# A turned tile read back from ScalarE's queue instead of SyncE's, with two other moves, in a two-layer decoder trunk

## What is computed

```
for l in range(2):
    x = LN1(alpha*x + 0.5*swiglu(x, ffn1_w_gate[l], ffn1_w_up[l], ffn1_w_down[l]))
    x = LN2(alpha*x + hybrid_mixer(x, w_in[l], ...))
    x = LN3(alpha*x + 0.5*swiglu(x, ffn2_w_gate[l], ffn2_w_up[l], ffn2_w_down[l]))

swiglu(x, g, u, d) = (silu(x @ g) * (x @ u)) @ d
```

## Time and profile before

| what | value |
|---|---|
| median of 3 runs | 1085.61 us (1084.34 to 1086.91) |
| profiled execution, its own time | 1085.02 us |
| its span | 1083.2 us |
| PE busy | 1074.1 us (99%) |
| VectorE busy | 772.2 us (71%) |
| ScalarE busy | 579.4 us (53%) |
| mean granted clock of TensorE | 0.998 |

### The profile page before, as it was taken

The page is one execution under the profiler, slowest core; times in us unless marked ns, Lnnn a source line. Parts: engine busy times, 40 slices in busy tenths (PEclk is TensorE's granted clock), DMA queues, the critical chain, the costliest instruction groups (busy, mean ns, idle before and its releaser), DMA issues.

```text
span 1083.2 us, 14466 instructions
## 1 busy us (share of the span) xinstructions
PE 1074.1 (99%) x5293; PEld 888.2 (82%) x5293; DVE 772.2 (71%) x773; ACT 579.4 (53%) x641; POOL 134.4 (12%) x137
## 2 busy tenths in 40 slices
PE   9999999999999999999999999999999999999997
PEld 6888888898888788888888888888988888888886
DVE  5747557799979775555679575677999787755566
ACT  5646654768555544444457555547774546444441
POOL 1397000000000000000006970000000000000000
PEclk9999999999999999999999999999999999999999
DMA  8767778355566477767737777785455674777771
GB/s 284 246 207 250 263 246 235 111 180 173 172 186 203 156 263 233 233 221 259 255 120 246 240 237 233 247 203 165 147 165 157 194 269 134 235 240 234 234 244 39
DMA packets 192371, 226.38 MB, mean 209 GB/s; under 512 B 31541, under 2 KB 157129, under 8 KB 192329
## 3 DMA queue, kind: packets, MB, share of 16 engines
q1 hardware_dynamic: 192328, 225.83, 65.5%
HBM read 214.26 MB, written 11.53 MB: 208 GB/s over the span
## 4 chain that ended last, share of the span: by engine, by line
PE 97%; DMA 1%; DVE 1%; ACT 0%; SPq 0%; issue 0%; DVEq 0%; ACTq 0%
PE ps L589 25%; PE ps L566 19%; PE ps L568 18%; PE ps L567 18%; PE ps L549 2%; PE ps L990 1%; PE ps L992 1%; PE ps L991 1%; PE ps L537 1%; PE ps L538 1%; PE ps L539 1%; PE ps L551 1%; PE ps L604 1%; PE ps L920 1%; PE ps L697 0%; PE ps L696 0%
## 5 line engine op out<-in xcount | busy, mean ns | idle before, releaser
L1471 DVE TENSOR_TENSOR w_lo<-raw,w_hi 128x2048 fp32r<-128x2048 f32 x172 | 399.8, 2328 | 167.7 <-ACT w_hi L1074 167.0
L1074 ACT CAST w_hi<-raw 128x2048 fp32r<-128x2048 f32 x172 | 328.2, 1911 | 170.4 <-PE ps L589 81.0
L566 PE MATMUL ps<-w_hi,xT 128*128 128x512 f32 x848 | 331.8, 391 | 0.3 <-DVE w_lo L1483 0.2
L567 PE MATMUL ps<-w_lo,xT 128*128 128x512 f32 x848 | 330.1, 389 | 0.0
L568 PE MATMUL ps<-w_hi,xT 128*128 128x512 f32 x848 | 330.1, 389 | 0.0
L566 PEld LDWEIGHTS ps<-w_hi,xT 128*128 128x128 f32 x848 | 159.2, 188 | 35.9 <-issue 2.5
L568 PEld LDWEIGHTS ps<-w_hi,xT 128*128 128x128 f32 x848 | 159.2, 188 | 33.5
L567 PEld LDWEIGHTS ps<-w_lo,xT 128*128 128x128 f32 x848 | 159.2, 188 | 32.6
L589 PE MATMUL ps<-w_hi,rows_hi 128*128 128x512 f32 x396 | 126.7, 393 | 0.3 <-DVE rows_lo L1520 0.2
L589 PE MATMUL ps<-w_hi,rows_lo 128*128 128x512 f32 x396 | 125.4, 390 | 0.0
L589 PE MATMUL ps<-w_lo,rows_hi 128*128 128x512 f32 x396 | 125.4, 389 | 0.0
(11 more groups left out here) (251 smaller groups left out, 1209.0 us busy)
## 6 DMA issues: line engine op xcount, KB each, us to landing
raw<-in_ffn_w_down SPq DMA_DIRECT2D x44, 1024.0 KB, 6.3
raw<-in_ffn_w_gate SPq DMA_DIRECT2D x86, 512.0 KB, 4.0
raw<-in_ffn_w_up SPq DMA_DIRECT2D x86, 512.0 KB, 5.2
raw<-in_w_in SPq DMA_DIRECT2D x30, 1024.0 KB, 5.1
hid_dram<-qT SPq DMA_DIRECT2D x160, 64.0 KB, 2.4
qT<-hid_dram SPq DMA_DIRECT2D x40, 256.0 KB, 2.6
raw<-in_w_out SPq DMA_DIRECT2D x8, 1024.0 KB, 4.8
raw<-in_w_in SPq DMA_DIRECT2D x8, 512.0 KB, 4.8
```

Source lines behind the costliest of these rows:

```text
L566: mm(o, xT[:, c, 0, tok], h, start=c == UPPER_FIRST[0], stop=False, skip_group_check=True)
L567: mm(o, xT[:, c, 0, tok], w, start=False, stop=False, skip_group_check=True)
L1074: nc.scalar.copy(w_hi[s][:, :], raw[s][:, :]).then_inc(hi_made.sem, 1)
L1471: tt(w_lo[s][:, :], raw[s][:, :], f32(w_hi[s][:, :]), ALU.subtract).then_inc(lo_made.sem, 1)
```

## The change

Three things are changed. (1) The read-back of the turned values is issued by ScalarE instead of SyncE. ScalarE waits for the four block writes and issues the DMA at the start of each step, ahead of the down chunk's cast; SyncE goes on from the block writes to the next load. (2) The loads of the norm's scale and shift move from behind the last loop of SyncE to between steps 7 and 8. (3) In the last step of an FFN the silu of the first token tile moves ahead of the cast of the next part's first chunk (`split_first`), where something follows.

```diff
                     sp.dma_start(hid_dram.rearrange("g i a r -> a i g r")[a],
                                  hid_blocks[32 * a:32 * a + 32, :].rearrange("i (g r) -> i g r", g=4)
                                  ).then_inc(blocks_out.sem, 16)
-                sp.wait_ge(blocks_out.sem, blocks_out.at(l, n))
-                sp.dma_start(hid_turned, hid_dram.rearrange("g i a r -> (g i) (a r)")).then_inc(h_turned.sem, 16)
...
                 after_steps()
-                with sp.Fori(5, STEPS) as i:
+                with sp.Fori(5, 8) as i:
                     step(i)
-                before_last()
+                norm_vectors()
+                with sp.Fori(8, STEPS) as i:
+                    step(i)
                 load(l, k0 + FFN_CHUNKS - 1, rows(w_down, l, DFF - 256))
                 turn_hidden(l, (f + 1) * (STEPS - 1))
...
+            def read_back(l, n):
+
+                sc_.wait_ge(blocks_out.sem, blocks_out.at(l, n))
+                nc.scalar.dma_start(hid_turned, hid_dram.rearrange("g i a r -> (g i) (a r)")).then_inc(h_turned.sem, 16)
+
...
                 def step(i):
+                    read_back(l, b0 + i)
                     split(l, k0 + i * 3 + 1, 1, LANDED[k0 + 1] + i * 16)
                     hidden_hi(l, b0 + i)
...
                 with sc_.Fori(2, STEPS - 1) as i:
                     step(i)
+                read_back(l, b0 + STEPS - 1)
...
                 split(l, k0 + FFN_CHUNKS - 1)
+                silu(l, s0 + STEPS, (half_used.sem, half_used.at(l, f + 1)), 4, slice(0, 1))
                 if following:
                     split_first(*following)
-                silu(l, s0 + STEPS, (half_used.sem, half_used.at(l, f + 1)), 4, slice(0, 1))
                 silu(l, s0 + STEPS + 1, pair(k0 + FFN_CHUNKS - 3), 4, slice(1, 2))
```

More of the change, by code:

```diff
@@ L366, in turn_hidden, with load_ffn @@
                                  ).then_inc(blocks_out.sem, 16)
-                sp.wait_ge(blocks_out.sem, blocks_out.at(l, n))
-                sp.dma_start(hid_turned, hid_dram.rearrange("g i a r -> (g i) (a r)")).then_inc(h_turned.sem, 16)
-            def load_ffn(l, f, w_gate, w_up, w_down, small, after_steps, before_last):
+            def load_ffn(l, f, w_gate, w_up, w_down, small, after_steps, norm_vectors):
                 k0 = FFN0[f]
```

## The result

The changed kernel takes 1113.42 us (median of 6 runs, 1111.3 to 1117.42), the kernel before beside it 1085.55 (6 runs, 1084.34 to 1086.91): ratio 1.0257, 95% interval 1.0242 to 1.0272, 27.9 us slower. The direction was predicted. The size was not: 10.5 us were forecast, and the range ended at 1103. The profiled execution of the changed kernel took 1117.42 us, 32.4 more than the profiled one of before, so what is read from it is somewhat too large for the median. The ratios leave out executions more than 1.5% above the fastest of the same kernel; there is one, of behind_cast (1121.26 us).

What follows compares the result with a forecast made beforehand. TensorE was taken as the bound, busy 1074.1 of 1083.2 us. Losses of 4.4 + 2.6 + 1.0 (VectorE beside GpSimd) + 0.8 + 0.6 + 0.8 + 0.3 made 10.5 us, so 1096 us, range 1090.5 to 1103.

Steps and rivals of the forecast that it cites:

- The order mechanism: ScalarE's queue: the wait for block writes now stands ahead of the down chunk's cast, making cast and low half late.
- term 2: Step 4 of each layer's first FFN: late down chunk delays small loads and block writes; 4.4 and 2.6 us.
- term 1: Step 1 of each FFN: down products start at W (block writes landed) + 5.5 us; 1.3, 0.8, 0.8, 0.6 later.
- Edits at nothing: Norm loads two and a half steps earlier and slot 0 weight loads 3 to 5 us sooner: no cost to PE.
- Term 3: FFN ends: silu moved up delays the next part's first cast, 0.8 us; last FFN's read-back delays a low half, 0.3.
- (b): TensorE's clock falls to 1.2 GHz after step 4's stall, costing 1.5 to 3 us: 1098 to 1099; 15 in 100.
- (e): Small loads 11.6 us, DMA issue over 1 us, or lateness handed on: 1100 to 1103, or 1105 and more; 11 in 100.
- (a): Only the FFNs' first steps cost, W of step 4 stays: 7.1 us, 1092; 17 in 100.
- (c): Faster: read-back lands sooner and weights come early, at most 0.7 us gained, 1084.9; 2 in 100.
- (d): No change: the block-write waits pass before ScalarE gets there; 5 in 100.

Runs made afterwards that it cites:

- behind_cast: Changed kernel, but ScalarE waits and issues the read-back behind the down chunk's cast, not ahead of it: 1110.48 us, ratio 1.0255.
- collision_only: Kernel before, but SyncE issues the slot 0 load ahead of its wait and read-back, ScalarE untouched: 1100.12 us, ratio 1.0129.
- Hold_cast_only: Kernel before, with ScalarE also waiting for the block writes ahead of the down chunk's cast; SyncE still reads back: 1099.24 us, ratio 1.012.
- norm_silu_alone: Kernel before, with only the norm loads and the silu moved up, read-back still on SyncE: 1085.08 us, ratio 0.9985.

## Why the prediction was wrong

**The step that failed** is the sentence "The read itself (2.66 us to the cast, from 27.72 to 30.38) now runs beside this and is hidden up to 3.6 us", and with it "the read gets no faster on ScalarE's queue, and this sum stands as it is". I asked what the read hides behind and whether it could become faster, but not what it would run beside. Of SyncE's loads of slot 0 I wrote "start 3 to 5 us sooner, but PE waits for no weight": I looked only at the consumer of these bytes. They moved from behind the read to ahead of it, and the read went from 2.6 to 4.4 us at the median, to 5.1 us up to the cast in the first step 1. In collision_only this one swap costs 14 us, more than the whole sum that I had. The rule that I cited, from the Trainium skill (DMA: Bandwidth & Descriptors, section "Issuing engines are not separate DMA queues"), says that such DMAs share 16 engines and interleave. The runs agree with it (behind 1 MB of loads the read takes 4.5 us from SyncE's queue and 4.4 to 4.5 from ScalarE's), and it speaks for the slower read: I took half of it.

**The order mechanism was right at step 4, and near the whole by luck.** Hold_cast_only has it alone and costs 13 us, against a sum of 10.5. At step 4 PE waits 3.16 and 2.86 us, 6.0 together; term 2 less the part of term 1 in it was 5.9. But the 3.5 us of term 1 are 1.0 there and the 0.8 for the silu has no place in a kernel without that move, while the rest of the 13 stands where the sum had no term: other steps, the last hidden values (1.8 us), and the clock (windows of 84 to 92 us: 0.69 and 0.88, some 1.6 us).

**Term 1** (1.3, 0.8, 0.8, 0.6). PE waits 2.07, 1.89, 1.93 and 1.88 us at the four places. From W to PE it took 6.6, 6.8, 6.5 and 6.9 us where I had 5.5; W itself was 0.35 earlier than before in the first. Each holds about a microsecond of late read. And it is the read that sets them, not the cast to which I charged them: with the order alone it is 5.0 us from W to PE at all four places and PE waits 1.0 us in total; with the collision alone it is 6.2 and 6.6 us in the first two, and PE waits 8.1 in the four.

**Term 2** (4.4 and 2.6, with 1.0 for VectorE). The mechanism is there. SyncE's queue in the changed kernel, from the down chunk of step 4 of the first FFN:

```profile
66.86 0.37 SPq L338 DMA_DIRECT2D raw<-in_ffn_w_down  x1
67.44 0.38 SPq L449 DMA_DIRECT2D S<-in_ssm_b_re  x1
...
75.61 1.85 SPq L364 DMA_DIRECT2D hid_dram<-qT  x4
```

and ScalarE, VectorE and PE behind the read-back:

```profile
81.29 0.33 ACTq L1112 DMA_DIRECT2D qT<-hid_dram  x1
...
81.79 1.28 ACT L1074 ACT_TABLE_LOAD   x1 [11.56 <-DMA hid_dram<-qT]
...
83.09 1.91 ACT L1074 CAST w_hi<-raw 128x2048 fp32r<-128x2048 f32 x1
...
87.26 1.75 DVE L1527 TENSOR_TENSOR rows_lo<-qT,rows_hi 128x512 fp32r<-128x512 f32 x1
...
89.15 1.19 PE L589 MATMUL ps<-w_hi,rows_hi 128*128 128x512 f32 x2 [4.77 <-DVE rows_lo L1527]
```

Down chunk 66.9 (forecast 65.4), small loads 67.4 (66.0), first write 75.6 (73.7), W 81.3 (78.8), PE 89.15 (85.6): 7.95 us behind the earlier trace rows in place of 4.4 (4.9 with the 0.5 for VectorE). Each part ran over a little. The start is 1.5 late, small loads take 8.2 us (7.7), the writes 5.7 (5.1), W to PE 7.9 (6.8). Of the last, 1.1 is VectorE's low part beside GpSimd, 1.75 us in place of 0.69. In layer 1 step 4 is 23.8 us behind the earlier trace rows where the step before it was 20.35 behind, so 3.4 for it, and 1.8 more in the step behind it.

**Edits at nothing.** The block writes were held to be untouched by the loads' new places; they take 3.7 us in place of 2.4. This may be why waits turn up in steps that I had passed over (0.45, 1.76 and 1.21 us in steps 3 and 5 and at 690 us); no run shows it by itself.

**Term 3** was 0.8 us of loss for the silu and 0.3 for the last FFN. The 0.8 are none; no run has the 0.3 by itself. The low half behind the silu starts 0.38 us later in norm_silu_alone (178.92 against 178.54; I had 0.45), but the turning products of the normalised rows, at which I had PE 0.3 later, start at 188.66 us against 188.65. The delay shrinks on VectorE's way there: 0.19 us at 181.86, 0.10 at 184.13, 0.02 at 186.99. So "VectorE works without a pause" was the wrong reading.

**Rivals.** (b) came true three times over (some 6 us against 1.5 to 3 for one), once behind step 4 as said and twice behind a step 1, beside everything else and not in place of it. (e), "much slower", names the right result with wrong causes: the small loads took 8.2 us and not 11.6, the issue 0.34 and not 1. Its third cause, lateness handed from step to step, is there only in part: behind step 4 of the first FFN the low part is ready again 0.46 to 3.5 us ahead of PE and PE's lag doesn't grow, while in the third FFN PE waits again in step 5 and at 690 us. (a), (c) and (d) are out.

**The sum**, in the profiled execution: 19.2 us of waits at down products, 3.0 at the last steps and the handover (2.5 and 0.5), 6.0 of clock make 28.2 of 32.4. PE's busy time is up by 9.5 us, 3.5 more than the clock explains, so most of the other 4 reads as busy PE and not as waits; I have not placed it.

## What to carry to other kernels

When a wait is taken from a queue that issues loads, list what that queue now issues ahead of the transfer that was waited for. The wait had a second use: it kept a megabyte out of the way of a short read whose latency is on the path (2.6 us without it, 4.4 with it). When a wait moves to a compute engine, price it by what stands behind it there, from the moment the wait ends; both effects can be tried alone in the old kernel with one line each. And a chain that meets an engine without idle time can cost twice, once in the wait and again in the clock behind it: three of the ten waits did here.

## What was not expected of the hardware

- A 256 KB read issued behind 1 MB of loads takes 4.5 us from its own issue when both are in SyncE's queue (collision_only), and 4.4 to 4.5 when the read is in ScalarE's (the changed kernel, behind_cast). A queue of its own gave it no way past the loads that these runs show. (In step 1 the loads were issued 1.9 and 1.4 us ahead of the read in the first case and 1.1 and 0.6 in the second, so a small gain from the own queue isn't excluded.) Behind 0.5 MB, in SyncE's queue, it is 3.9; behind nothing it is 2.6 to 2.8 from either queue.
- The clock fell behind waits of PE of 1.89 and 1.93 us (second and third FFN), but not behind those of 2.07 and 1.88 (first and fourth) nor behind one of 3.3. The length of a single wait doesn't tell it. Nor did it fall in these two waits: in half-microsecond windows it was still at 1.00 when PE began again at 398.49 and 584.97, and was at 0.50 from 399.0 and was at 0.50 from 399.0 and from 586.5 on, with PE busy. In the wait of 4.77 us it had fallen while PE stood (0.54 from 88 to 89 us).
